# In-projections with the last 128 tokens as the stationary side, an end stored in column parts, and finer orders at the hand-overs

## What is computed

```python
def layer_a(x, h0, mk, mv, w_in, w_out, ...):
    u, gate, mq, mg = _split_proj(rms_norm(x, g_pre) @ w_in)      # 2048 -> 1536 + 1536 + 512 + 512
    y, h_last = s5_scan(u, h0, ...)                                 # diagonal SSM, 96 groups of 16
    y = gelu(y); y = y * sigmoid(y @ w_glu + b_glu)
    a_out = y * silu(gate)
    m_out = mem_attention(mq, mk, mv) * silu(mg)                    # 4 heads, 256 memory rows
    return x + rms_norm(concat([a_out, m_out]) @ w_out, g_post), h_last

k, v = split(rms_norm(x, g_kv) @ w_kv)                              # after layer a, once

def layer_b(x, k_all, v_all, q_offset, mk, mv, w_in, w_out, ...):
    q, gate, mq, mg = _split_proj(rms_norm(x, g_pre) @ w_in)
    o = stick_breaking_attention(q, k_all, v_all, q_offset)         # 12 heads of 128
    ... gated, joined with memory attention, w_out, norm, residual
```

## Time and profile before

| | us |
|---|---|
| median of 3 runs | 2251.62 (2251.11 to 2253.45) |
| profiled execution | 2251.52 |
| its span | 2249.8 |
| TensorE busy | 2198.5 (98%) |
| VectorE busy | 1099.2 (49%) |
| ScalarE busy | 870.4 (39%) |
| GpSimd busy | 320.8 (14%) |
| mean granted clock of TensorE | 0.995 |

### The profile page before, as it was taken

One profiled execution on the slowest core, in us unless ns is written; L12 is line 12 of the kernel. 1 busy time (PEld: TensorE's weight loads), 2 busy tenths in 40 slices (PEclk: granted clock), 3 DMA queues, 4 the chain that ended last, 5 costly groups with the idle time before them and its releaser, 6 DMA issues.

```text
span 2249.8 us, 36227 instructions
## 1 busy us (share of the span) xinstructions
PE 2198.5 (98%) x13866; PEld 1991.8 (89%) x13866; DVE 1099.2 (49%) x1871; ACT 870.4 (39%) x1665; POOL 320.8 (14%) x481
## 2 busy tenths in 40 slices
PE   8999999999999999999999999999999999899997
PEld 6789999999999998887788888999999999888886
DVE  5659889898745363224312212345444444562223
ACT  4543332333445352224222222456565654552221
POOL 1621202211111000002100000122122212010001
PEclk9999999999999999999999999999999999999999
DMA  7724434434644334224233333444444445344223
GB/s 272 231 80 109 111 106 109 123 103 122 225 133 143 108 103 177 75 75 159 83 100 98 114 106 98 144 148 132 135 132 146 132 136 202 121 156 168 83 77 140
DMA packets 176970, 293.45 MB, mean 130 GB/s; under 512 B 25428, under 2 KB 104960, under 8 KB 173440
## 3 DMA queue, kind: packets, MB, share of 16 engines
q1 hardware_dynamic: 132720, 159.32, 23.6%
q0 software_dynamic: 25168, 92.92, 13.4%
q10 hardware_dynamic: 19008, 40.18, 4.8%
HBM read 243.75 MB, written 48.61 MB: 130 GB/s over the span
## 4 chain that ended last, share of the span: by engine, by line
PE 93%; DVE 2%; DMA 1%; ACT 1%; POOL 1%; issue 1%; SPq 0%; ACTq 0%; POOLq 0%; DVEq 0%
PE PS L207 15%; PE PS L208 15%; PE PS L209 15%; PE PS L1447 11%; PE PS L1448 11%; PE PS L1449 11%; PE PS L541 1%; PE PS L821 1%; PE PS L536 1%; PE PS L1639 1%; PE PS L1640 1%; PE PS L1641 1%; PE PS L1179 1%; PE PS L1151 1%; PE PS L513 1%; PE PS L1476 1%
## 5 line engine op out<-in xcount | busy, mean ns | idle before, releaser
L207 PE MATMUL PS<-XH,WH 128*128 128x320 f32 x2336 | 736.1, 315 | 4.6 <-DVE XL L1516 1.4
L209 PE MATMUL PS<-XH,WL 128*128 128x320 f32 x2336 | 723.0, 310 | 0.0
L208 PE MATMUL PS<-XL,WH 128*128 128x320 f32 x2336 | 722.8, 309 | 0.0
L189 DVE SCALAR_TENSOR_TENSOR WL<-RAW,vec,WH 128x256 fp32r<-128x256 f32 (+1 forms) x608 | 281.4, 523 | 499.5 <-ACT WH L175 495.1
L1447 PE MATMUL PS<-WH,XH 128*128 128x512 f32 x1168 | 457.0, 391 | 7.3 <-DVE WL L189 3.4
L1448 PE MATMUL PS<-WL,XH 128*128 128x512 f32 x1168 | 456.0, 390 | 0.0
L1449 PE MATMUL PS<-WH,XL 128*128 128x512 f32 x1168 | 456.0, 390 | 0.0
L207 PEld LDWEIGHTS PS<-XH,WH 128*128 128x128 f32 x2336 | 439.8, 188 | 15.5 <-issue 8.5
L208 PEld LDWEIGHTS PS<-XL,WH 128*128 128x128 f32 x2336 | 440.0, 188 | 0.2
L209 PEld LDWEIGHTS PS<-XH,WL 128*128 128x128 f32 x2336 | 439.6, 188 | 0.0
L175 ACT ACTIVATE WH<-RAW,vec 128x256 fp32r<-128x256 f32 (+1 forms) x608 | 281.8, 534 | 347.3 <-DMA RAW<-in_w_kv_dram 175.8
(11 more groups left out here) (306 smaller groups left out, 2076.5 us busy)
## 6 DMA issues: line engine op xcount, KB each, us to landing
RAW<-in_w_in_a_dram SPq DMA_DIRECT2D x64, 512.0 KB, 4.0
RAW<-in_w_in_b_dram SPq DMA_DIRECT2D x64, 512.0 KB, 3.8
RAW<-in_w_kv_dram SPq DMA_DIRECT2D x48, 512.0 KB, 3.6
RAW<-in_w_out_a_dram SPq DMA_DIRECT2D x32, 512.0 KB, 3.8
RAW<-in_w_out_b_dram SPq DMA_DIRECT2D x32, 512.0 KB, 3.8
scratch_in_a<-EST ACTq DMA_DIRECT2D x32, 320.0 KB, 3.7
RAW<-in_w_glu_dram SPq DMA_DIRECT2D x24, 384.0 KB, 3.3
scratch_in_b<-EST ACTq DMA_DIRECT2D x26, 320.0 KB, 3.2
```

What stands on the lines that cost most here:

```text
L189: ins = eng.scalar_tensor_tensor(out=wview(WL, slot, ph)[:, kt, :], in0=wview(RAW, slot, ph)[:, kt, :], scalar=vec[:, g:g + 1], in1=wview( ...
L207: pe.matmul(acc, wh, xh, start=first, stop=False)
L208: pe.matmul(acc, wh, xl, start=False, stop=False)
L209: return pe.matmul(acc, wl, xh, start=False, stop=last)
```

## The change

**In-projections.** A new form of a unit, `unit_mixed`, for all of in_a and for chunks 0 to 12 of in_b. The last 128 of the 640 tokens (from `HEAD` = 512) are held stationary and 256 weight columns move past them, into bank 0; then for each of the two column blocks the weights are stationary and the 512 other tokens move, into banks 1 and 3. In a chunk's last unit bank 0 (tokens by columns) has been copied to `EST`, and TensorE turns it back, two blocks of 128x128, into bank 2, before the last three matmuls. `store_blocks` empties in the order 0, 1, 2, 3 and stores both row blocks at the end.

```diff
+        def unit_mixed(pe, ph, U, k, n, between=None, ready=None):
...
+            hook(0)
+            bank_free(0)
+            for kt in range(ph.kts):
+                xh, xl = XH[:, k * ph.kts + kt, HEAD:TOK], XL[:, k * ph.kts + kt, HEAD:TOK]
+                first, last = k == 0 and kt == 0, whole and kt == ph.kts - 1
+                pe.matmul(PS[:, 0, 0:2 * P], xh, wh[:, kt, 0:2 * P], start=first, stop=False)
+                pe.matmul(PS[:, 0, 0:2 * P], xh, wl[:, kt, 0:2 * P], start=False, stop=False)
+                ins = pe.matmul(PS[:, 0, 0:2 * P], xl, wh[:, kt, 0:2 * P], start=False, stop=last)
+            if whole:
+                ins.then_inc(s_bank[ph.name], 1)
+            hook(1)
+            for m in range(2):
+                bank_free(1 + 2 * m)
+                for kt in range(ph.kts):
+                    if kt == ph.kts - 1 - m:
+                        hook(2 + m)
+                    if whole and m == 1 and kt == ph.kts - 1:
+                        pe.wait_ge(s_ev[ph.name], 4 * n + 1)
+                        pe.transpose(PS[:, 2, 0:P], EST[:, 0, HEAD:TOK], ident[:])
+                        pe.transpose(PS[:, 2, P:2 * P], EST[:, 1, HEAD:TOK], ident[:]).then_inc(s_bank[ph.name], 1)
+                    x = (slice(None), k * ph.kts + kt, slice(0, HEAD))
+                    w = (slice(None), kt, slice(m * P, m * P + P))
+                    ins = three(pe, PS[:, 1 + 2 * m, 0:HEAD], wh[w], wl[w], XH[x], XL[x], k == 0 and kt == 0, whole and kt == ph.kts - 1)
```

```diff
@@ ScalarE
                     mem_act(act, 1, mem_unit(n, k), (0,))
                     ahead(split_high, act, ph, U, k)
+                    mem_act(act, 1, mem_unit(n, k), (1,))
...
-                    mem_act(act, 1, mem_unit(n, k), (1, 2, 3))
+                    mem_act(act, 1, mem_unit(n, k), (2, 3))
```

```diff
+            for t in range(NT - 1):
+                sp.wait_ge(s_x1, NT + t + 1)
+                sp.dma_start(out["y_prompt"][0, P * t:P * t + P, :], OUTROW[:, t, :]).then_inc(s_yout, 16)
+            for p in range(4):
+                c = slice(p * D // 4, (p + 1) * D // 4)
+                sp.wait_ge(s_x1, 2 * NT + p)
+                sp.dma_start(out["y_sample"].rearrange("b i d -> (b i) d")[:, c], OUTROW[:, NT - 1, c]).then_inc(s_yout, 16)
+            sp.wait_ge(s_yout, 16 * (NT + 3))
...
-                dst = out["y_prompt"][0, P * t:P * t + P, :] if t < NT - 1 else out["y_sample"].rearrange("b i d -> (b i) d")
-                pool.dma_start(dst, OUTROW[:, t, :]).then_inc(s_yout, 16)
-            pool.wait_ge(s_yout, 16 * NT)
```

More of the change, by code:

```diff
@@ L1429, in unit_stationary, with hook, bank_free @@
                     ins.then_inc(s_bank[ph.name], 1)
+        def unit_mixed(pe, ph, U, k, n, between=None, ready=None):
+            pe.wait_ge(s_wl, U + 1)
+            pe.wait_ge(s_wh, U + 1)
+            wh, wl = wview(WH, k % RING, ph), wview(WL, k % RING, ph)
+            whole = k == ph.upc - 1
+            def hook(q):
+                if between:
+                    between(q)
+            def bank_free(b):
+                if k == 0 and not (isinstance(n, int) and n == 0):
+                    pe.wait_ge(s_ev[ph.name], 4 * n - 3 + b)
+                elif ready:
+                    ready(b)
+            hook(0)
[21 more added lines that the diff above has]
+                    ins = three(pe, PS[:, 1 + 2 * m, 0:HEAD], wh[w], wl[w], XH[x], XL[x], k == 0 and kt == 0, whole and kt == ph.kts - 1)
+                if whole and m == 0:
+                    ins.then_inc(s_bank[ph.name], 1)
+            ins.then_inc(s_wu, 1)
         def unit_moving(pe, ph, U, k, n, tiles, fill=None, bank=0, sets=1, ready=None, only=None):
@@ L1587, in chunk @@
                     unit_stationary(pe, ph, ph.upc * n + ph.first + k, k, n)
-            chunk(ph, 0)
+            for x in range(ph.upc):
+                pe.wait_ge(s_xl, 25 + x)
+                unit_mixed(pe, ph, ph.first + x, x, 0)
             with pe.Fori(0, BATCHES) as i:
@@ L1683, in _ @@
             ph = phases["in_b"]
-            first_chunk(ph, "kv", 26)
+            for x in range(ph.upc):
+                unit_mixed(pe, ph, ph.first + x, x, 0, ready=(lambda b: pe.wait_ge(s_ev["kv"], 26 + b)) if x == 0 else None)
             pe.wait_ge(s_ev["kv"], 30)
@@ L1752, in _ @@
                 turned_high(act, t + 2)
+            ahead(split_high, act, ph, ph.first + 4 * ph.upc - 1, ph.upc - 1)
             ph = phases["in_a"]
             def store_blocks(name, n, col, q):
-                m, h = q // 2, q % 2
                 ph = phases[name]
-                if h == 0:
-                    if not (isinstance(n, int) and n == 0):
+                if q == 0 and not (isinstance(n, int) and n == 0):
+                    for m in range(2):
                         act.wait_ge(s_st[name][m], n * 16)
                 bank_full(act, ph, n, q, 4)
-                act.activation(EST[:, m, h * HALF:h * HALF + HALF], PS[:, q, 0:HALF], ACT.Copy).then_inc(s_ev[name], 1)
-                if h == 1:
+                if q % 2 == 0:
+                    act.activation(EST[:, :, HEAD:TOK], PS[:, q, 0:2 * P].rearrange("p (m c) -> p m c", m=2),
+                                   ACT.Copy).then_inc(s_ev[name], 1)
+                else:
+                    act.activation(EST[:, q // 2, 0:HEAD], PS[:, q, 0:HEAD], ACT.Copy).then_inc(s_ev[name], 1)
+                if q >= 2:
+                    m = q - 2
                     act.wait_ge(s_ev[name], n * 4 + q + 1)
@@ L1997, in _ @@
                 turned_low(dve, t + 2)
+            ahead(split_low, dve, ph, ph.first + 4 * ph.upc - 1, ph.upc - 1)
             def chunk(ph, n, aux=()):
@@ L2074, in residual @@
                 k = 5 + 10 * l + t
-                dve.scalar_tensor_tensor(out=OUTROW[:, t, :], in0=OUTROW[:, t, :], scalar=rstd[:, k:k + 1], in1=RES[slot],
-                                         op0=ALU.mult, op1=ALU.add).then_inc(s_x1, 1)
+                parts = 4 if (l, t) == (1, NT - 1) else 1
+                for p in range(parts):
+                    c = slice(p * D // parts, (p + 1) * D // parts)
+                    dve.scalar_tensor_tensor(out=OUTROW[:, t, c], in0=OUTROW[:, t, c], scalar=rstd[:, k:k + 1], in1=RES[slot][:, c],
+                                             op0=ALU.mult, op1=ALU.add).then_inc(s_x1, 1)
             def diagonal(t):
@@ L2109, in _ @@
             diagonal(4)
-            turned_low(dve, 11)
             ph = phases["kv"]
-            with dve.Fori(0, 5) as i:
+            for k in range(ph.upc):
+                ahead(split_low, dve, ph, ph.first + k, k)
+                if k == 1:
+                    turned_low(dve, 11)
+            with dve.Fori(1, 5) as i:
                 chunk(ph, i)
@@ L2127, in _ @@
                     j = BRANCH_AT.index((n, k)) if (n, k) in BRANCH_AT else None
+                    ahead(split_low, dve, ph, ph.upc * n + ph.first + k, k)
+                    if n == 13 and k == 0:
+                        mem_queries_dve(dve, 1)
                     if j is not None:
@@ L2134, in _ @@
                         dve.tensor_tensor(AM[:, kb, :], AM[:, kb, :], GB1[:], ALU.mult).then_inc(s_gd, 1)
[L2135 to L2137 removed]
+                    mem_dve(dve, mine, 1, mem_unit(n, k), (2, 3))
                     if j is not None:
```

31 lines of the change are left out of this document (15 added, 16 removed).

## The result

The changed kernel takes 2225.13 us (median of 4 runs, 2224.89 to 2226.11) where the kernel before takes 2251.36 (4 runs, 2250.09 to 2253.45): a ratio of 0.9883, 95% interval 0.9866 to 0.9901, so 26.2 us less. Forecast were 2222.1 (2211 to 2238). The profiled execution of after took 2226.11 (span 2224.4), 25.4 us less than that of before; the 25.4 are what the traces can be asked about.

A forecast was written before the change was run, and what follows sets the result against it. TensorE, busy 98% of the span, was taken to bound the kernel. Terms -18.6 + 8.4 + 1.3 + 0.8 + 1.2 - 3.1 - 7.4 - 6.7 - 5.3 gave -29.4 from 2251.5: 2222.1 us, range 2211 to 2238.

The forecast's parts named there:

- Matmuls, -18.6: In-projections: 116 units with twelve fewer matmuls each, 6.88 us for 7.04, 18.6 us less.
- Rival (d): In-projections: loading the stationary side is the floor, 256 columns take 146.7 ns; 37.2 us more, 2259.3; chance 3%.
- rival (b): In-projections: the fixed part per matmul doesn't go with the count, so 18.6 is lost; 2240.7 us; chance 7%.
- SSM loop, +1.2: SSM loop: VectorE nearly as long as TensorE, slack 0.6 us; a 0.2 us wait in each of 6 batches, 1.2 more.
- Chunks 13 and 15, +1.3: In_a: turns wait about 0.9 us for ScalarE in chunk 13, units at chunk 15's end gain nothing (0.4); 1.3 more.
- First head, +0.8: First head's queries: two stores leave together at a chunk's end, so TensorE's 1.9 us wait grows by about 0.8.
- Memory to in_a, -3.1: Start of in_a: first unit waits only for a quarter of the last rows; 1.4 wait and 1.7 half clock go.
- Out_a to kv, -7.4: Row-2 copies before row 4's residual, kv splits earlier: waits shrink by 2.3 and 3.4 us, half clock of 1.7 goes.
- End of in_b, -6.7: Turned blocks copied before the gate wait: late-copy waits of 5.3 and 1.0 us and a half clock go, less new waits.
- Tail, -5.3: Program's end: last residual in four pieces stored by SyncE, GpSimd's drain beside them; close at 2244.5 for 2249.8 us.
- Rival (c): Hand-overs: waits only change their releaser, nothing left of -3.1, -7.4 and -6.7; 2239.3 us; chance 8%.
- rival (a): Hand-overs: long waits go but the half clocks stay at three places, 5.1 us more, 2227.2; chance 12%.

The follow-up runs named there:

- turns_twice: The changed kernel with each pair of turns made twice, into the same bank; 2229.43 us (one run).
- v_early: The changed kernel, with both halves of the SSM loop's V products 9 wide matmuls earlier in their unit; 2222.81 us, 0.9874 of the kernel before.
- orders_old_units: The changed kernel with the old units of 48 matmuls of 320 everywhere, new hand-over orders and tail kept; 2231.34 us, 0.9903 of the kernel before.
- last_row_whole: The changed kernel, but SyncE stores the last row whole, after one residual; 2227.76 us, 0.9886 of the kernel before.
- parts_by_gpsimd: The changed kernel, but GpSimd issues all stores of y, the last row in its four parts; 2231.26 us, 0.9903 of the kernel before.
- units_alone: The kernel before with the mixed units alone, old hand-over orders and old tail; 2249.30 us, 0.9986 of the kernel before.

## Why the prediction was right, and where it was wrong

The direction and the size came out: 25.4 against a forecast 29.4 on the profiled executions. By its terms:

- **Matmuls, -18.6.** The price held: 119 ns at 256 columns, 228 at 512, a unit 6.90 for 6.88. So an undisturbed unit saves 0.14 in place of 0.16, 16 us in 116. Rival (d) (a load floor, from 141 ns) and rival (b) (the fixed part stays) fall. The Trainium skill, TensorE: Matmul & The Clock Gate, section "Wait — 56ns, not 53.3ns?", has a fixed cost of about 2.5 ns; with it 256 columns would come to about 109 ns here (an estimate), and the trace disagrees: the third width lies on the line with 13.4, in a stream of fp32r matmuls that each have a load of their own.
- **Turns, +8.4.** Priced a little high: 0.22 a pair by the rows and 0.24 by doubling them.
- **Units and turns together** should have been 4 x 0.16 - 0.29 = 0.35 a chunk. Where neither copies nor VectorE hold TensorE up, in in_b's loop, a chunk went from 37.36 to 37.12: 0.24, or 1.3 us less than forecast in twelve. Four units at 0.14 less a pair at 0.23 would give 0.33; no wait stands in that loop, so the missing 0.1 must lie where a chunk is broken into by fp32 matmuls. After the turns the first wide matmul takes 0.31 us to the next in place of 0.23; behind a block in before a 320 took 0.23 in place of 0.147. No run isolates what a break costs each form.
- **SSM loop, +1.2.** This step failed most. It forecast a batch shorter by some 0.5 us net (eight units, two pairs, 0.2 of waiting); it is 0.09, so 2.5 us are missing. The mechanism was named, VectorE's chain with a slack of 0.6. But the step measured that slack at the states, where it was 0.46, and left out that VectorE's later steps of the batch, on which the next batch's first turn waits, are shifted with them. There before had almost none: the three additions take 1.75 us in before, held up by TensorE's last products, and 1.61 in after, so 0.14 is all that could be saved behind the V products. And the 0.4 that the products' later place saves behind them is lost ahead of them, where the units' gain should have shown: 23.50 us became 23.54. 0.14 less 0.04 is, but for rounding, the 0.09 measured. turns_twice and v_early show the chain to be the length.
- **Chunks 13 and 15, +1.3.** The wait of L1477 in chunk 13 is 1.07 (0.9 forecast). A second one, 0.55 in chunk 15, wasn't forecast; the wait of 0.8 for VectorE's fills that stood behind that chunk in before is gone, so there the units earn little, as the prediction had it with 0.4.
- **First head, +0.8.** The wait grew by 0.5. The half clock behind it, 1.7, was not in the sum. It isn't the units' doing: orders_old_units has it without them. It comes in some executions.
- **Memory to in_a, -3.1.** The lead at the SSM loop is 5.3. The wait of 1.4 went as forecast, and with it the half clock of before's trace; about 2 more come from the memory stage, where before had a stall of 2.9 and a half clock and this execution had a shorter stall and none. That part is chance: traces of the new order have the stall too (3.2 in last_row_whole).
- **Out_a to kv, -7.4.** Measured: 11.4 - 5.5 = 5.9 up to the unit that had waited, and 13.0 - 11.4 = 1.6 for the half clock behind it: 7.5.
- **End of in_b, -6.7.** The lead grows by 6.2. The waits on copies went, the new ones came: 1.3 for a copy (0.7 forecast), 1.0 for the bank (0.9), 1.2 left of the wait for EST (1.1).
- **Tail, -5.3.** Measured 5.3. parts_by_gpsimd and last_row_whole show both causes that the prediction named, the drain as the larger one.

Rival (c), that hand-over waits only change their releaser, falls with the lead table, though no run takes out one hand-over's order alone; rival (a) falls for the three places it spoke of: none of the eleven traces with the new orders has a half clock there. What their going is worth is less sure than the sum had it, though. Of the two traces with the old orders and waits, only before has the half clocks at 125 and 1934 us; units_alone has none there. So part of the 5.1 hangs on what the profiled execution of before happened to have. Of the sum's excess of 4.0 us, the SSM loop is 2.5, the chunks of in_b 1.3, the half clock 1.7 and the end of in_b 0.5; the memory stage gives back 2.0, by chance. Of the signs that the prediction named, three failed: the batch is 0.09 us shorter and not 0.4 to 0.8, TensorE waits for EST in two chunks and not in one, and a half clock stands ahead of the end.

## What to carry to other kernels

Where a loop runs through two engines in turn, measure the time of the other engine's piece in the trace, to the last step that anyone waits for: what is saved beside it is lost once its slack is gone, and moving the point at which it starts (v_early) gives back what a cheaper stream could not. Look at the hand-overs and the last microseconds first: here orders of copies and splits, and the choice of the engine that stores last, gave about six times what a better shape of 116 units did (orders_old_units is 21.1 us under before, units_alone 3.2). And compare stages by the starts of the same instruction: a median can hide a gain of 4 us behind a stall in another stage.

## What the runs showed of the hardware

- GpSimd's drain at the program's end takes 3.58 us (before) and 3.82 (parts_by_gpsimd) where all its stores have landed before it starts, and 3.79 in after, where it stores nothing of y; SyncE's takes 0.013.
- A half clock of 3.4 us behind a wait of about 2 us is not certain. For the first head's queries it came after waits of 1.98, 2.19, 2.35, 2.42, 2.45, 2.53 and 2.54 us, and not after 1.91, 2.29, 2.34 and 2.45; where the wait was taken away, it never came (two traces).
- Two turns of 128x128 in plain fp32, read from what ScalarE has just copied, cost a stream of wide matmuls 0.22 us (after) to 0.24 (turns_twice).
